# A hybrid decoder trunk: attention scores with the keys on the partitions, and the residual kept in DRAM

## The reference

```python
def causal_block_attention(q, k, v, log_decay_cum=None):      # q, k: (1, 1024, 8, 64 or 96), v: (1, 1024, 8, 64)
    for blk in range(T // Q_BLOCK):                           # 128 queries
        s = jnp.einsum('bqhd,bkhd->bhqk', q[:, lo:hi], k[:, :hi]) * scale
        if log_decay_cum is not None:                         # fox only
            s = s + (cum[:, :, lo:hi, None] - cum[:, :, None, :hi])
        p = jax.nn.softmax(jnp.where(mask, s, -jnp.inf), axis=-1)
        outs.append(jnp.einsum('bhqk,bkhd->bqhd', p, v[:, :hi]))
...
y = jnp.concatenate([ya, yb, yc, yd], axis=-1).astype(proj.dtype) * jax.nn.silu(gate)
return x + (y @ w_out).astype(x.dtype)
```

## Time and profile before

| | |
|---|---|
| median of 3 runs | 3226.34 us (3224.7 to 3227.0) |
| profiled execution, its span | 3222.3 us |
| PE busy | 2601.3 us, 81% |
| DVE busy | 1357.5 us, 42% |
| ACT busy | 867.1 us, 27% |
| POOL busy | 468.7 us, 15% |
| granted TensorE clock, mean | 0.904 of full speed |

### The profile page before, as it was taken

One profiled execution on the slowest core, in us unless ns is written; L12 is line 12 of the kernel. 1 busy time (PEld: TensorE's weight loads), 2 busy tenths in 40 slices (PEclk: granted clock), 3 DMA queues, 4 the chain that ended last, 5 costly groups with the idle time before them and its releaser, 6 DMA issues. The chain is left out here.

```text
span 3222.3 us, 36887 instructions
## 1 busy us (share of the span) xinstructions
PE 2601.3 (81%) x14416; PEld 2124.9 (66%) x14416; DVE 1357.5 (42%) x2296; ACT 867.1 (27%) x1389; POOL 468.7 (15%) x308
## 2 busy tenths in 40 slices
PE   4976678998987898985868776889989878889766
PEld 3855568787766666773657555777877757677545
DVE  3119931522532545515231397225235336364153
ACT  3023310322311424305131233113123124342041
POOL 1115521010020000110111254210100200001111
PEclk9988989999988999998978888889999889999888
DMA  3000010000010000001010000100000100000102
GB/s 114 14 29 1 1 53 15 14 27 27 1 35 25 14 9 14 14 27 30 27 61 14 29 1 3 51 15 14 27 27 2 34 25 14 9 14 14 43 13 79
DMA packets 74534, 78.65 MB, mean 24 GB/s; under 512 B 16080, under 2 KB 63344, under 8 KB 74352
## 3 DMA queue, kind: packets, MB, share of 16 engines
q1 hardware_dynamic: 74352, 76.19, 7.5%
HBM read 71.99 MB, written 4.19 MB: 24 GB/s over the span
## 5 line engine op out<-in xcount | busy, mean ns | idle before, releaser
L892 PE MATMUL psum<-gla_ql,gla_kl 128*128 128x256 f32 x448 | 143.8, 476 | 102.6 <-DVE gla_ql L687 102.5
L892 PEld LDWEIGHTS psum<-gla_ql,gla_kl 128*128 128x128 f32 x448 | 104.4, 243 | 146.5 <-DVE gla_A L759 107.8
L484 DVE TENSOR_TENSOR x_res<-x_res,psum 128x512 f32<-128x512 f32 x128 | 86.0, 685 | 194.0 <-PE psum L503 193.8
L1106 DVE TENSOR_REDUCE fox_nmax<-psum 128x1 f32<-128x128 f32 (+7 forms) x128 | 97.0, 758 | 137.1 <-PE psum L1039 136.4
L1106 DVE TENSOR_REDUCE mla_nmax<-psum 128x1 f32<-128x128 f32 (+7 forms) x128 | 97.0, 758 | 136.6 <-PE psum L1039 135.8
L1125 ACT ACTIVATE mla_q<-psum,mla_nmax 128x128 f32<-128x128 f32 (+7 forms) x128 | 94.8, 741 | 205.6 <-DVE mla_nmax L1106 205.6
L1125 ACT ACTIVATE fox_qa<-psum,fox_nmax 128x128 f32<-128x128 f32 (+7 forms) x128 | 94.8, 741 | 205.6 <-DVE fox_nmax L1106 205.6
L1036 PE MATMUL psum<-fox_kT,fox_qT 66*128 66x512 f32 (+3 forms) x384 | 149.8, 500 | 0.0
L1036 PE MATMUL psum<-mla_kT,mla_qT 96*128 96x512 f32 (+3 forms) x384 | 149.8, 500 | 0.0
L1059 PE MATMUL psum<-fox_v,fox_ka 128*128 128x64 f32 x1152 | 142.7, 270 | 0.0
L1059 PE MATMUL psum<-mla_v,mla_k 128*128 128x64 f32 x1152 | 142.7, 270 | 0.0
(11 more groups left out here) (369 smaller groups left out, 5611.9 us busy)
## 6 DMA issues: line engine op xcount, KB each, us to landing
w_next<-in_w_in_dram SPq DMA_DIRECT2D x26, 1024.0 KB, 5.2
w_next<-in_w_out_dram SPq DMA_DIRECT2D x8, 1024.0 KB, 5.1
fox_w_raw<-in_w_in_dram SPq DMA_DIRECT2D x6, 1024.0 KB, 7.2
x_res<-in_x_dram SPq DMA_DIRECT2D x1, 4096.0 KB, 12.6
gla_w_raw<-in_w_in_dram SPq DMA_DIRECT2D x4, 1024.0 KB, 6.9
out_dram<-x_res SPq DMA_DIRECT2D x1, 4096.0 KB, 11.7
gla_w_raw<-in_w_in_dram SPq DMA_DIRECT2D x2, 1088.0 KB, 5.2
fox_w_raw<-in_w_in_dram SPq DMA_DIRECT2D x2, 1056.0 KB, 9.6
```

The costliest lines, as they stand in the source:

```text
L484: dve.tensor_tensor(at, at, k.psum[:, u % 8, :], ALU.add).then_inc(added, 1)
L892: last = pe.matmul(k.psum[:, n % NB, g * HH * HALF:(g + 1) * HH * HALF], kl[:, m % RING, g, :], ql[:, m % RING, g, :, :] .rearrange("p h t ...
L1106: dve.tensor_reduce(nmax[:, u:u + 1], score_ap(u), AX_X, ALU.max, negate=True)\
```

## The change

The stage becomes one block. Items are two pairs of heads by two halves of the queries (512). For an item's units (a block of 128 keys and one of the two heads) PE makes the scores turned, keys on partitions and up to 512 queries moving, as three rounded products, adds the mask turned, and ACT exponentiates straight into the P that the P V product takes as its moving side, with 64 columns of v stationary and two heads in the two halves of one bank. The row maximum has to be known first: one rounded product with queries on partitions gives it, DVE reduces it, PE turns it and ACT writes it as an extra row 0 of q's rounded part (k has ones there). Row sums: POOL adds the P tiles up, a product with ones sums them over partitions, ACT and DVE invert them, POOL multiplies the gate by them, DVE by the output. q and k are turned in groups of four within the stage, those of the second pair beside the first pair's second item. P V of a unit stands two units behind its scores. The residual is no longer in SBUF: setup copies x to the output in DRAM, the norm loads it, and the output block loads, adds and stores its 16 tiles of 256 KB through six buffers. Layouts of q and k change from token, head to head, token, with one more column.

Cut to its core (semaphore lists, allocations and layout edits of copies are left out):

```diff
-                sp.dma_start(k.x[:, :, :], d["x"][0].rearrange("(t p) n -> p t n", p=P)).then_inc(loaded, 16)
+                sp.dma_start(k.out[0].rearrange("(t p) n -> p t n", p=P), d["x"][0].rearrange("(t p) n -> p t n", p=P)).then_inc(loaded, 16)
...
+                sp.dma_start(x[:, :, :], k.out[0].rearrange("(t p) n -> p t n", p=P)).then_inc(x_landed, 16)
...
+                act.wait_ge(x_landed, 16)
...
+                for i in range(len(units) + 3):
+                    if i < len(units):
+                        if i >= XR:
+                            sp.wait_ge(x_stored[i % XR], 16 * (i // XR))
+                        sp.dma_start(xt[:, i % XR, :], rows(i)).then_inc(x_in[i % XR], 16)
+                    if i >= 3:
+                        u = i - 3
+                        sp.wait_ge(added, u + 1)
+                        sp.dma_start(rows(u), xt[:, u % XR, :]).then_inc(x_stored[u % XR], 16)
+                for i in range(XR):
+                    sp.wait_ge(x_stored[i], 16 * len(range(i, len(units), XR)))
...
+                    dve.wait_ge(x_in[u % XR], 16 * (u // XR + 1))
                     dve.wait_ge(unit_done, u + 1)
-                    at = k.x[:, t, half(n)]
+                    at = xt[:, u % XR, :]
...
+    def unit(self, i, j):
+        kb = j // 2
+        return kb, j % 2, max(0, kb * P - self.items[i][1] * BANK)
+    def pre_at(self, i, j):
+        p, c = self.items[i]
+        return (p + 1, j) if c == 1 and p + 1 < self.NP and j < 8 else None
+    def scores_at(self, i, j):
+        if i + 1 == len(self.items):
+            return range(0)
+        if self.items[i][1] == 0:
+            return range(3 * j, min(3 * j + 3, 16)) if j < 6 else range(0)
+        return range(2 * (j - 8), 2 * (j - 8) + 2) if 8 <= j < 12 else range(0)
+    def m_at(self, i, j):
+        if i + 1 == len(self.items):
+            return None
+        return {5: 0, 7: 1}.get(j) if self.items[i][1] == 0 else {12: 0, 13: 1}.get(j)
...
+        def misc_wait(*use):
+            m = self.misc[use]
+            if m >= 2:
+                sem, n = self.misc_end[m - 2]
+                pe.wait_ge(sem, n)
+        def turn(p, g):
+            src, _, _, _, h, c = self.group(p, g)
+            misc_wait("pre", p, g)
+            for x in range(4):
+                last = pe.transpose(k.psum[:D, self.misc_bank("pre", p, g), x * P:(x + 1) * P], src[:, h, 4 * c + x, :],
+                                    k.ident[:, :])
+            last.then_inc(self.turned, 1)
...
+        def score(i, n):
+            p, c = self.items[i]
+            a, qt, part, lo, hi = self.score(i, n)
+            u, h = self.s_base[i] + n, 2 * p + a
+            if n == 0:
+                pe.wait_ge(self.hi_done, 8 * p + 4 * (c + 1))
+            if u >= 2:
+                pe.wait_ge(self.max_done, u - 1)
+            out = k.psum[:, 2 + u % 2, :hi - lo]
+            diagonal = hi == (qt + 1) * P
+            last = pe.matmul(out, self.q_hi[:, h, qt * P:(qt + 1) * P], self.k_hi[:, h, lo:hi], start=True,
+                             stop=not diagonal)
+            if diagonal:
+                last = pe.matmul(out[:, hi - lo - P:], k.ident_bf[:, :], k.mask_bf[:, :], start=False, stop=True)
...
+        def turned_scores(i, j):
+            p, c = self.items[i]
+            kb, a, lo = self.unit(i, j)
+            u, h = self.t_base[i] + j, 2 * p + a
+            if j == 0:
+                pe.wait_ge(self.lo_done, 8 * p + 4 * (c + 1))
+            if j < 2:
+                pe.wait_ge(self.m_done, 2 * i + a + 1)
+            if u >= 2:
+                pe.wait_ge(self.exp_done, u - 1)
+            out = k.psum[:, u % 2, lo:]
+            keys, queries = slice(kb * P, (kb + 1) * P), slice(c * BANK + lo, (c + 1) * BANK)
+            pe.matmul(out, self.k_hi[:, h, keys], self.q_hi[:, h, queries], start=True, stop=False)
+            pe.matmul(out, self.k_hi[:, h, keys], self.q_lo[:, h, queries], start=False, stop=False)
+            diagonal = kb >= 4 * c
+            last = pe.matmul(out, self.k_lo[:, h, keys], self.q_hi[:, h, queries], start=False, stop=not diagonal)
+            if diagonal:
+                last = pe.matmul(k.psum[:, u % 2, lo:lo + P], k.mask_bf[:, :], k.ident_bf[:, :], start=False, stop=True)
+            last.then_inc(self.st_done, 1)
+        def pv(i, j):
+            p, c = self.items[i]
+            kb, a, lo = self.unit(i, j)
+            u, h = self.t_base[i] + j, 2 * p + a
+            pe.wait_ge(self.exp_done, u + 1)
+            if j == 0 and i >= 2:
+                pe.wait_ge(self.y_done, i - 1)
+            pe.matmul(k.psum[a * HEAD:(a + 1) * HEAD, 4 + i % 2, lo:], self.v[:, kb, h * HEAD:(h + 1) * HEAD],
+                      self.p[u % self.PR][:, lo:], start=(kb == 0), stop=(kb == 4 * c + 3)).then_inc(self.pv_done, 1)
+        def row_sums(i):
+            misc_wait("rs", i, 0)
+            pe.wait_ge(self.acc_done, self.t_base[i + 1])
+            for a in range(2):
+                last = pe.matmul(k.psum[a * HEAD:(a + 1) * HEAD, self.misc_bank("rs", i, 0), :], self.ones[:, :],
+                                 self.acc[:, i % 2, a, :], start=True, stop=True)
+            last.then_inc(self.rs_done, 1)
...
+        warm_clock(k, pe, 7)
+        for g in range(4):
+            turn(0, g)
+        for n in range(8):
+            score(0, n)
+        for g in range(4, 8):
+            turn(0, g)
+        for a in range(2):
+            turn_max(0, a)
+        late = []
+        for i in range(len(self.items)):
+            for j in range(self.n_units(i)):
+                turned_scores(i, j)
+                late.append((i, j))
+                if len(late) > 2:
+                    pv(*late.pop(0))
+                if self.pre_at(i, j) is not None:
+                    turn(*self.pre_at(i, j))
+                for n in self.scores_at(i, j):
+                    score(i + 1, n)
+                if self.m_at(i, j) is not None:
+                    turn_max(i + 1, self.m_at(i, j))
+                if i and j == 3:
+                    row_sums(i - 1)
+        pv(*late[0])
+        pv(*late[1])
+        row_sums(len(self.items) - 1)
...
+        def round_group(p, g):
+            _, hi, _, gain, h, c = self.group(p, g)
+            act.wait_ge(self.turned, 8 * p + g + 1)
+            act.activation(hi[:, h, c * BANK:(c + 1) * BANK], k.psum[:D, self.misc_bank("pre", p, g), :], ACT.Copy,
+                           scale=gain[:, 0:1]).then_inc(self.hi_done, 1)
+        def place_max(i, a):
+            p, c = self.items[i]
+            act.wait_ge(self.m_turned, 2 * i + a + 1)
+            act.activation(self.q_hi[0:1, 2 * p + a, c * BANK:(c + 1) * BANK], k.psum[0:1, self.misc_bank("m", i, a), :],
+                           ACT.Copy).then_inc(self.m_done, 1)
+        def exponent(i, j):
+            _, _, lo = self.unit(i, j)
+            u = self.t_base[i] + j
+            act.wait_ge(self.st_done, u + 1)
+            if u >= self.PR:
+                act.wait_ge(self.pv_done, u - self.PR + 1)
+                act.wait_ge(self.acc_done, u - self.PR + 1)
+            act.activation(self.p[u % self.PR][:, lo:], k.psum[:, u % 2, lo:], ACT.Exp).then_inc(self.exp_done, 1)
+        def invert(i):
+            act.wait_ge(self.rs_done, i + 1)
+            if i >= 1:
+                act.wait_ge(self.u_done, i)
+            act.activation(self.r0[:, :], k.psum[:, self.misc_bank("rs", i, 0), :], ACT.Ln).then_inc(self.ln_done, 1)
+            act.wait_ge(self.ln_done, i + 1)
+            act.activation(self.r0[:, :], self.r0[:, :], ACT.Exp, scale=-1.0).then_inc(self.r0_done, 1)
...
+                exponent(i, j)
+                if self.pre_at(i, j) is not None:
+                    round_group(*self.pre_at(i, j))
+                if self.m_at(i, j) is not None:
+                    place_max(i + 1, self.m_at(i, j))
+                if i and j == 4:
+                    invert(i - 1)
...
+        def rest_of_group(p, g):
+            _, hi, lo, gain, h, c = self.group(p, g)
+            at = slice(c * BANK, (c + 1) * BANK)
+            dve.wait_ge(self.hi_done, 8 * p + g + 1)
+            dve.scalar_tensor_tensor(out=lo[:, h, at], in0=k.psum[:D, self.misc_bank("pre", p, g), :],
+                                     scalar=gain[:, 0:1], in1=hi[:, h, at].bitcast(F32), op0=ALU.mult,
+                                     op1=ALU.subtract).then_inc(self.lo_done, 1)
...
+        def maximum(i, n):
+            c = self.items[i][1]
+            a, qt, part, lo, hi = self.score(i, n)
+            u = self.s_base[i] + n
+            dve.wait_ge(self.scores, u + 1)
+            x = qt - 4 * c
+            if c and n % 8 == 0 and i >= 2:
+                dve.wait_ge(self.max_joined, 2 * (i // 2 - 1) + a + 1)
+            out = self.nm2[:, a, x, part:part + 1] if c else self.nmax[:, i, a, x:x + 1]
+            dve.tensor_reduce(out, k.psum[:, 2 + u % 2, :hi - lo], AX_X, ALU.max, negate=True).then_inc(self.max_done, 1)
```

(95 more changed lines are left out.)

344 lines of the change are left out of this document (161 added, 183 removed).

## The result

The changed kernel takes 3618.16 us (median of 4 runs, 3604.33 to 3624.44) against 3225.52 before (4 runs): 1.1212 times, 95% interval 1.1189 to 1.1234, slower. The forecast was 3391 and the range ended at 3515: the direction was right, and the loss is 393 us where 165 were forecast. The profiled execution has a span of 3618.5 against 3222.3.

The account below looks back on a forecast made before the run. TensorE (PE) was taken to bound the kernel, busy 96.0 of 100.0 us in each of eight attention stages. From 3222.3, +124 for the stages and +41 for the residual gave 3387, 3391 us as a median; range 3310 to 3515.

Parts of the forecast that it names:

- the half clock: Start of each attention stage: TensorE, idling there, loses clock and runs its work slower; 3 us a stage (0 to 7).
- PE's work, 81.7 for 80.4: TensorE's work in an attention stage: 81.7 us removed, 80.4 added, 91.1 in all with what stays.
- rival D: Attention stages: gaps smaller than counted, row sums' pairs overlapped (-3.4); -12 us a stage, 3295 us; chance 12%.
- Start: Start of each attention stage: TensorE waits on transposes, their evacuation and the maxima; 8.9 us idle a stage.
- Rival A: P V in attention stages: TensorE empties at each change of width; 15.4 us a stage, +123, 3514 us; chance 12%.
- Middle: The four items of an attention stage: TensorE waits for banks, maxima and row sums; 5.5 us lost (0 to 12).
- End: End of each attention stage: last addition, row-sum inversion, gate and final product uncovered; 6.2 us idle, 1.6 before.
- Rival B: Attention stages: GpSimd, adding the P tiles, becomes the bound; +5 us a stage, 3431 us; chance 10%.
- Rival C: P V in attention stages costs TensorE little, running beside its neighbours; half hidden 18.9 us a stage, 3240; chance 4%.
- Residual, +41: Residual in DRAM: norm loads 23, output stores 24, semaphores 3.5 and 1, setup 3, last store removed 13.2; +41 us.

Follow-up runs that it names:

- filler: The changed kernel with 29 rounded full-array products a stage added where TensorE waits at the start of an attention stage: 3618.72 us.
- fox97: The changed kernel with fox's q and k padded by zeros from 66 to 97 entries, P tiles placed as in mla: 3537.95 us.
- mla66: The changed kernel with mla's score products on the first 66 of their 97 rows: 3725.5 us.
- pv128: The changed kernel with P V's stationary 128 columns wide instead of 64, so the output is not the attention's: 3439.29 us.
- pairs: The changed kernel with P V products issued two and two, both heads of a key block one behind the other: 3441.77 us.
- best: The changed kernel with P V issued two and two, fox padded to 97 entries, and filling products at the stage's start: 3328.02 us.
- resid_dram: The kernel before with only the residual's edits (residual in DRAM), on the old attention: 3267.89 us against 3223.89, 1.0136 times.

## Why the prediction was right or wrong

Direction and bound were right: the stages are PE's, its work was traded almost one for one, and the residual cost what was said. Two terms of a stage's sum failed: the half clock, counted with 3 us, and the pause around each P V, which the sum had at nothing and a rival at 12%. By the account below they miss 107 and 98 us of the eight stages. Added to the forecast alone, either would have left the time in the stated range (3498 or 3489); both together did not.

*PE's work, 81.7 for 80.4: held.* Rounded products of 128 columns stand 0.11 apart (759.75 to 759.86 in the changed kernel), float32 P V costs 0.86 without its pauses (1.56 less three times 0.23). One term was too high: the row sums' two products run side by side, both heads in 1.08 us (L1147 below), as rival D had it, 3.4 a stage less than counted.

*Start: held in kind.* The sum put it at 18.8 us (9.9 of work, 8.9 idle), the slow clock left aside; with the clock mostly held (*filler*) it is 20.0 in fox and 21.3 in mla, +1.8 in the mean, the added products in it. ACT's rounding took 0.69, as forecast, and DVE's rest 0.75 for 0.69:

```profile
L1234 DVE SCALAR_TENSOR_TENSOR fox_q_lo<-psum,fox_q_gain,fox_q_hi 66x512 fp32r<-66x512 f32 x32 | 23.9, 746 | 98.3 <-ACT fox_q_hi L1185 98.3
```

*The half clock, 3 us a stage (0 to 7): the first step that failed.* It took for granted that the clock is lost only where PE idles, and that only the start idles. In mla that was nearly so: 5.7 us a stage (134.4 less 128.7). In fox it cost another 21.2 a stage (155.7 less 134.4), with PE busy 28.9 of 30.0 us, because the score products stand on 66 rows of the array; *fox97* and *mla66* show it both ways, and *pv128* that P V's 64 columns have a share in it. No row of before warned of it: there the 66-row products were 31 us of float32 among 47 of products with full rows, at a clock of 1.00. In the changed kernel P V, on 64 columns, takes the place of those full products, and the 66-row ones are rounded; of the two only P V's width was tried (*pv128*), and it counts. The Trainium skill (TensorE: Matmul & The Clock Gate, Part 1) has the clock follow how busy PE has been; here the records show PE 96% busy and the clock at its lower level, and zeros in 31 more rows lift it. The measurement decides: in these stages being busy was not enough to bring the clock up, and more rows in the same products brought it up in most of them.

*Rival A, 12%: it happened, and its term was missing from the sum.* The pause is 0.35 us a unit of 512, 12.3 us a stage, against 15.4 worked out there. It was set aside because transposes with 66 columns run like full ones; but in the rows of before those stand among their own kind, while P V on half the columns stands between products on all of them. The Trainium skill (TensorEngine Tiling (Array Packing), Key Properties) says that a change of mode drains TensorE; *pv128* and *pairs* agree: the pause goes with the width, and a pair of units has 0.37 us of it (2.61 less six times 0.23 and 0.86) where two units had 0.70.

*Middle, 5.5: the waits held, PE's work behind the start was priced too low.* Behind the start a stage of mla at full clock takes 107.4 in *filler*, forecast 92.9 (91.1 less the start's 9.9, and 5.5 and 6.2). Of these 14.5, 12.3 are pauses; 3.4 come off for the row sums and 1.1 for the end; 6.7 are left. They are not waits, for up to the last record of P V and row sums PE idles 5.25 us, about what was forecast:

```profile
1248.30:1350.60 102.30, 97.05 (x408) 47.41 (x406) 35.60 (x61) 35.53 (x70) 46.89 (x51) 1.00 0.00 1
```

Part of it shows in the distances of starts: a rounded product of 512 columns whose predecessor is a mask or a transpose lasts 0.31 to 0.34 until the next start, not 0.23 (1266.24 to 1266.55 in *filler*; 1198.96 to 1199.27 in *pv128*, so it isn't among the pauses that P V's width makes). 36 products of this stretch, of all widths, stand so, 3.6 us in all by their distances. Why, and where the other 3.1 are, no run took apart.

*End, 6.2:* 5.1. Last row sums, ACT, DVE, POOL and DVE in the order forecast:

```profile
761.20 1.08 PE L1147 MATMUL psum<-fox_acc,fox_ones 128*64 128x512 f32 x4 [0.19 <-POOL fox_acc L1302]
762.31 0.60 ACT L1207 ACTIVATE fox_r<-psum 128x512 f32<-128x512 f32 x1 [1.79 <-PE psum L1147]
...
766.46 0.69 DVE L1268 TENSOR_TENSOR fox_gate<-psum,fox_gate 128x512 f32<-128x512 f32 x1 [1.44 <-POOL fox_gate L1308]
```

Over eight stages: pauses 98, fox's clock 85, the clock at the start 8 x (5.7 - 3) = 22, start 14, middle 54, row sums -27, end -9: +237 over the forecast's 124, and 361 were measured. The middle's 54 is what is left over, so the sum closes by construction.

*Rival B, GpSimd:* didn't happen. A 512 addition took 1.30 (forecast 1.27), POOL is busy 48 us of an mla stage of 134, and PE waits for it 0.19 us at the end:

```profile
L1302 POOL TENSOR_TENSOR fox_acc<-fox_acc,fox_p 128x512 f32<-128x512 f32 x64 | 83.2, 1302 | 71.3 <-ACT fox_p L1201 70.9
```

*Rival C, P V beside its neighbours:* not in the changed kernel, for the reason given (two P V never stand together). *pairs* shows that the order alone withheld it, but even *best* stays on the slower side.

*Residual, +41:* 44.0 by *resid_dram*. Norm +24.3 (forecast 23) by the lengths of its two blocks, with ACT waiting for x 12 us each time; output blocks +29.8 in eight (forecast 27.5 with their semaphores); setup +1.6 (3); last store -12.0 (13.2). The source view of the norm's squares in the changed kernel, and the page's DMA issues:

```profile
  DMA norm_x<-out_dram: 24.0, 2
```

```profile
norm_x<-out_dram SPq DMA_DIRECT2D x2, 4096.0 KB, 13.1
...
gla_xt<-out_dram SPq DMA_DIRECT2D x32, 256.0 KB, 5.1
out_dram<-gla_xt SPq DMA_DIRECT2D x32, 256.0 KB, 3.0
```

The 3.0 us taken for a last store's landing is what the page shows.

## What to carry to other kernels

Count a product's place on the array, not only its columns: here a 64-column stationary between full ones cost 0.35 us a unit, and two such products on different halves, issued back to back, took the time of one. When a rewrite puts most of the time into products on part of the array, look at the granted clock where PE is busy before blaming waits; padding with zeros took 80 us off here, without changing a result. And a kernel whose bound engine trades 82 us of work for 80 has nothing to pay new waits with: the start and the end of each stage, and the residual's landings, were lost before the clock came into it.

## What the runs showed of the hardware that was not expected

- TensorE at 1.2 GHz (0.50) for 51 us on end in the first fox stage while busy 48.6 of them, and for 78.5 us in a stage of *filler* while busy 77.6 of them, with rounded products on 66 rows and P V on 64 columns; at 2.4 GHz in most of the same order of work with 97 rows. Products on all rows and columns in front of it (*filler*) don't prevent it; P V on 128 columns instead of 64 (*pv128*) mostly does, even with 66 rows.
- The clock is not the same in equal stages: fox stages of one execution took 150.7 and 173.4 us (*filler*), 133.3 and 142.9 (*fox97*), while the mla stages of these executions agree within 0.4.
- Two float32 products of 512 columns on different column halves: 1.01 us for both, against 1.00 for one with its pauses.
